# Sample attention in a decoder step: first values load issued ahead of the last unit's stores, last merge one entry later

## The reference

```python
def dilated_attn_sample(q, kv_all, past_rows, window, dil):
    ...
    s = jnp.einsum('bshe,bskhe->bshk', q, g[:, :, :, 0]).astype(jnp.float32) * ATTN_SCALE
    p, lse = masked_softmax_stats(s, valid[None, :, None, :])
    o = jnp.einsum('bshk,bskhe->bshe', p.astype(q.dtype), g[:, :, :, 1])
    return o, lse

def merge_dilation_groups(outs, lses):
    w = jax.nn.softmax(jnp.stack(lses, axis=0), axis=0)
    o = jnp.einsum('gblh,gblhe->blhe', w, jnp.stack(outs, axis=0).astype(jnp.float32))
```

## Time and profile before

| | |
|---|---|
| median of 3 runs | 2883.84 us |
| lowest, highest | 2879.44, 2885.67 us |
| span of the profiled execution | 2888.2 us |
| PE busy in it | 2766.8 us (96%) |
| DVE, ACT, POOL busy | 1331.5, 832.1, 822.3 us |
| DMA | 301.82 MB, mean 105 GB/s |

### The profile page before, as it was taken

How to read it: one execution, slowest core, us unless ns; L and a number is a source line. 1 busy time by engine, 2 the same in 40 slices (tenths; PEclk the granted TensorE clock), 3 DMA queues, 4 the chain that set the end, 5 groups by cost and what they waited for, 6 DMA issues and landing times.

```text
span 2888.2 us, 47476 instructions
## 1 busy us (share of the span) xinstructions
PE 2766.8 (96%) x18529; PEld 2633.0 (91%) x18529; DVE 1331.5 (46%) x2462; ACT 832.1 (29%) x1952; POOL 822.3 (28%) x505
## 2 busy tenths in 40 slices
PE   7999999999999999999999988989999999999997
PEld 5988998898899799999999977789999999999997
DVE  5477468647756851222323223277733333333334
ACT  5453154135325502323333322233400000000004
POOL 2342334324233423212212121123131313131322
PEclk9999999999999999999999998999999999999998
DMA  6533544333354431123232269972111111111111
GB/s 205 171 107 122 163 122 147 110 131 107 122 163 127 149 109 46 46 54 90 52 85 58 68 192 268 279 228 106 30 52 37 52 37 52 37 52 37 52 49 67
DMA packets 340262, 301.82 MB, mean 105 GB/s; under 512 B 25592, under 2 KB 308776, under 8 KB 338704
## 3 DMA queue, kind: packets, MB, share of 16 engines
q1 hardware_dynamic: 255744, 242.30, 27.6%
q10 hardware_dynamic: 84296, 56.40, 6.7%
HBM read 249.49 MB, written 102.91 MB: 122 GB/s over the span
## 4 chain that ended last, share of the span: by engine, by line
PE 85%; DVE 3%; DMA 3%; ACT 2%; issue 2%; SPq 2%; POOL 1%; ACTq 1%; DVEq 0%; POOLq 0%
PE ps L2145 23%; PE ps L2146 22%; PE ps L2147 22%; PE ps L2471 2%; PE ps L2447 2%; DMA kraw<-in_cache_kv_w_dram 1%; PE ps L2313 1%; PE ps L2309 1%; PE ps L2462 1%; PE ps L2153 1%; PE ps L2515 1%; PE ps L2154 1%; PE ps L2155 1%; PE ps L2312 1%; DMA wraw<-in_w_out_dram 1%
## 5 line engine op out<-in xcount | busy, mean ns | idle before, releaser
L2145 PE MATMUL ps<-hH,wH 128*128 128x384 f32 (+1 forms) x1896 | 636.1, 336 | 16.2 <-issue 5.2
L791 POOL CAST wH<-wraw 128x1024 fp32r<-128x1024 f32 (+2 forms) x186 | 195.1, 1049 | 1521.7 <-PE ps L2147 1164.1
L2146 PE MATMUL ps<-hL,wH 128*128 128x384 f32 (+1 forms) x1896 | 622.1, 328 | 0.0
L2147 PE MATMUL ps<-hH,wL 128*128 128x384 f32 (+1 forms) x1896 | 622.1, 328 | 0.0
L793 POOL TENSOR_TENSOR wL<-wraw,wH 128x1024 fp32r<-128x1024 f32 (+2 forms) x186 | 447.8, 2407 | 14.9
L2145 PEld LDWEIGHTS ps<-hH,wH 128*128 128x128 f32 x1896 | 359.3, 189 | 32.9 <-issue 23.3
L2145 PE MATMUL ps<-mH,wH 128*128 128x384 f32 (+1 forms) x1128 | 371.3, 329 | 3.6 <-issue 3.6
L2146 PE MATMUL ps<-mL,wH 128*128 128x384 f32 (+1 forms) x1128 | 370.8, 329 | 0.0
L2147 PE MATMUL ps<-mH,wL 128*128 128x384 f32 (+1 forms) x1128 | 370.2, 328 | 0.0
L2146 PEld LDWEIGHTS ps<-hL,wH 128*128 128x128 f32 x1896 | 359.5, 190 | 0.0
L2147 PEld LDWEIGHTS ps<-hH,wL 128*128 128x128 f32 x1896 | 358.8, 189 | 0.0
(11 more groups left out here) (386 smaller groups left out, 5038.6 us busy)
## 6 DMA issues: line engine op xcount, KB each, us to landing
wraw<-in_w_in_dram SPq DMA_DIRECT2D x92, 512.0 KB, 3.9
wraw<-in_w_up_dram SPq DMA_DIRECT2D x44, 512.0 KB, 3.7
ssdcr<-cum_scr ACTq DMA_DIRECT2D x32, 512.0 KB, 4.8
out_dram<-in_cache_kv_w_dram SPq DMA_DIRECT2D x16, 960.0 KB, 5.3
wraw<-in_w_down_dram SPq DMA_DIRECT2D x22, 512.0 KB, 3.2
kraw<-in_cache_kv_w_dram SPq DMA_DIRECT2D x40, 256.0 KB, 8.6
vraw<-in_cache_kv_w_dram SPq DMA_DIRECT2D x40, 256.0 KB
ssds<-in_state_ssm_dram ACTq DMA_DIRECT2D x16, 512.0 KB, 4.2
```

Source lines behind the costliest of these rows:

```text
L791: pool.tensor_copy(hi, a).then_inc(w_hi, 1)
L2145: pe.matmul(dst, hi, cols(mH[:, k, :], c), start=k == 0, stop=False)
L2146: pe.matmul(dst, hi, cols(mL[:, k, :], c), start=False, stop=False)
L2147: last = pe.matmul(dst, lo, cols(mH[:, k, :], c), start=False, stop=k == kt - 1)
```

## The change

Three things move; nothing is added to the work or taken from it, except one more wait on SP.

1. On SP, `load_v(0)` with its waits stands ahead of `send_unit(NJ - 1, 2)` and `merge_store(2)` instead of behind them. `load_new(0)` stays behind the stores, with an explicit wait for them.
2. `merge_load(NJ - 1)` moves from before entry 0's `load_new` to behind entry 2's K. The merge's steps on DVE and its exponential on ACT, which were in the second and third entry (`b` 1 and 2), come one entry later.
3. The load of `atok` from `a_scr` moves from behind entry 1's K to behind entry 4's K, that is, into the fourth pass of the loop. `load_gate_chunk(7)` stays where it was.

```diff
                     for y in range(3, 7):
                         load_gate_chunk(y)
-                    send_unit(NJ - 1, 2)
-                    merge_store(2)
                     sp.wait_ge(s_ready, tiles)
                     sp.wait_ge(vt_ready, tiles)
                     sp.wait_ge(kvn_out[1], 16 * 2)
                     load_v(0)
-                    merge_load(NJ - 1)
+                    send_unit(NJ - 1, 2)
+                    merge_store(2)
+                    sp.wait_ge(unit_out[2], 16 * 6 * NJ + 1)
                     load_new(0)
                     for b in range(DB - 1):
                         sp.wait_ge(k_fill, 12 * b + 9)
                         load_k(b + 1)
                         if b == 0:
+                            load_gate_chunk(7)
+                        if b == 1:
+                            merge_load(NJ - 1)
+                        if b == 3:
                             sp.wait_ge(pv_ready, tiles)
                             sp.wait_ge(a_out, 16 * (NJ - 1))
                             for j in range(NJ - 1):
                                 sp.dma_start(atok[:, :, j * P:(j + 1) * P], a_scr[j]).then_inc(at_in, 16)
-                            load_gate_chunk(7)
@@ ACT
-                if b == 1:
+                if b == 2:
                     merge_exp(NJ - 1)
@@ DVE, ahead of the wait for the exponential
-                if b == 1:
+                if b == 2:
                     merge_ops(NJ - 1, 1, 3)
-                if b == 2:
+                if b == 3:
                     merge_ops(NJ - 1, 9, 11)
```

## The result

The changed kernel takes 2865.58 us (median of 17 runs, 2859.16 to 2877.3) against 2885.67 us for the kernel before (median of 17 runs beside them). The ratio is 0.994, with a 95% interval of 0.9927 to 0.9952: 17 us faster, between 14 and 21. That is inside the range of the prediction and 4 us better than its number, -13.

A forecast was written before the change was run, and what follows sets the result against it. PE bounds nearly the whole span, but sample attention begins bound by transfers. Entry by entry -16.3 us, -12 with slower loads, taken as -13: 2870.8 us against the median 2883.84; range 2862 to 2879 for 8 in 10 runs.

The forecast's parts named there:

- The idle stretch and the first wait: Ahead of entry 0: DMA queue idle 12 us, then full; early values block starts the values product at 1722.6, not 1735.03: -12.4 us.
- The worst case for `vnew`: Entry 0: `vnew` takes 7.9 us as in a full queue, lands at 1726.5, gain 8.5 us instead of 12.4.
- The walk: Sample attention followed entry by entry with 8.4 us a load: -21.3 us at entry 2's keys, -16.3 at entry 4.
- a new wait in entry 3: Entry 3's keys land at 1772.3, behind the moved `mgb`; PE asks at 1767.7: a wait of 4.6 us.
- the wait for `pts`: PE's 1.98 us wait while DVE's merge products run beside POOL's split; moves from entry 2 to entry 3, size kept.
- POOL's quarter: DVE's three merge products, run alone, gain the same quarter as POOL's split (2.40 for 3.23): 4.8 us.
- The sum: Whole change: -16.3 us with loads of 8.4 us, -12 with slower transfers; -13 taken, so 2870.8 us.
- The queue has more room: Sample attention: entry 3's keys not late, products free of POOL, -21 to -23 us kept, 2863 to 2861; chance 0.12.
- Most is given back: DMA queue full from 1720 to entry 7's keys: gain only -4 to -9 us, 2875 to 2880; chance 0.18.
- The early block delays something: Last unit's stores late by 8.4 us: entry 0's gain shrinks to 4 us, no change, 2880; chance 0.04.
- DVE waits for the late `mgb`: Entry 2: late `mgb` holds DVE, then PE; gain used up if 16 us late; 2884 to 2892; chance 0.04.
- The rule beside the sum: Loads at about 358 GB/s per core: a block takes 6.6 us, no new wait arises, result about -20 us.

## Why the prediction was right, step by step

**The idle stretch and the first wait.** Right in what the sum used. (The worst case for `vnew`, given as 1726.5, is 1717.6 + 7.9 = 1725.5, and its gain 9.5 instead of 8.5; the sum doesn't use it.) The wait of 12.42 us is gone (the values product starts 16.2 us after the first keys; 1722.6 - 1706.28 = 16.3 were forecast). The trace has no landing time for the value block, but the queue was full up to the first store, at 1701.05, and not beyond: the DMA share is 1.03 from 1698 to 1700, 0.78 from 1700 to 1701 and 0.42 from 1701 to 1703. The stores were not late: DVE's wait for them ended 11.2 us after the first keys, 11.3 before. `vnew`, which was given up to 4 us in the worst case, cost nothing.

**The walk.** Time of each entry's first keys, counted from entry 0's (us; the last column is the product behind the stage):

| | entry 1 | entry 2 | entry 3 | entry 4 | entry 7 | next stage |
|---|---|---|---|---|---|---|
| before | 37.2 | 63.6 | 86.1 | 105.1 | 167.4 | 192.9 |
| forecast by the walk | 23.0 | 42.3 | 66.0 | 88.8 | 153.7 ("near 1860") | - |
| after, first profile | 22.4 | 43.8 | 68.0 | 91.6 | 150.6 | 175.5 |
| after, second | 24.1 | 43.2 | 66.5 | 89.0 | 153.9 | 181.0 |
| after, third | 23.0 | 43.6 | 67.1 | 89.4 | 155.9 | 181.4 |

The order of gains and debts is as forecast: a peak in entry 2, a new wait in entry 3 (4.6 forecast; 5.12, 4.08 and 4.45 measured), the wait for `pts` moved to entry 3 (1.98 forecast; 1.83 in all three). The run with the products in entry 4 shows the one debt to be POOL's split beside DVE, the run with `mgb` one entry on the other to be `mgb`'s place. One price in the walk was off: for the three products alone it had 4.8 us, from POOL's quarter, and they took 3.50.

**The sum.** The walk gave -16.3; I took 3 us off for a slower queue and said -13. This is the step that was mis-sized. The timed difference is -17 (14 to 21), so the walk's own number was the better one. The stretch from 1710 to 1770 ran at 290 GB/s (282 and 287 in the other two profiles), not at 271. The 271 of the earlier trace rows is a mean over a stretch that also holds the end of the unit's stores, and I had used it for loads of K and V: in the same trace of the kernel before, 1720 to 1780, past the stores and with `atok` still inside, has 282. The 240 GB/s taken for `mgb` and `atok` stands in no row of any run; with `mgb` inside, 1725 to 1765 of the changed kernel has 290. The profiles don't settle the rest. At entry 4 the three have -13.5, -16.1 and -15.8, at the next stage -17.5, -12.0 and -11.5: what differs is how long entries 6 and 7 wait for keys, 0.8 to 7.7 us in sum, in one and the same kernel. The assumption that both kernels wait the same there can be neither shown nor denied from one profile each.

**The rivals.** "The queue has more room" is off: the keys of entry 3 were late in every profile. "Most is given back" (-4 to -9) is off too, at -17. "The early block delays something" had no trace in any row. "DVE waits for the late `mgb`" did not happen: DVE began L1797 the moment its reduction was done. Something else that I did not foresee sits there, below. The rule beside the sum finds no support where it was applied: while the loads of keys and values fill the queue, the changed kernel's best row had 318 GB/s (1830 to 1860), and the new wait that the rule would have denied arose. In other traffic the rate was higher: 351 GB/s from 1850 to 1880 in the run with `atok` last, where gates, weights and `accm` are loaded too. The rule is that of the Trainium skill, HBM Reference, section Specifications (TRN2), with about 358 GB/s per core.

**Which part brought it.** By the timed runs the value block is worth 7.5 us alone, `mgb` and `atok` together 10.7, `atok` in that 4 to 8. The rival of the given-back gain called the block of 2.36 MB the only real gain in bytes; that is right for a queue that is full to the end, but `mgb` and `atok` also left the full stretch for the middle one, where the share rose from 0.84 to 0.95.

## What to carry to other kernels

Where the profile shows an engine waiting for a transfer, look past the named one to what stands ahead of it in the queue, and look for an idle stretch of the same queue right before: a block moved there alone was worth about its own length here (7.5 us for 8.4), and a walk entry by entry with one measured load time forecast the next four entries within 3 us. Inside the full stretch, moving `mgb` one entry on only moved the wait, and spreading it gave nothing that could be measured. Whether taking bytes out of the stretch helps by itself is not shown: the two runs that did so can't be told from the change by their times, and only the third, which also put the next stage's weights first, is likely ahead of it. It pays to look at who is next in line, since a stage that ends earlier also asks earlier for what stands behind it. Where two profiles of one kernel differ by as much as the step that is judged, only the timed runs decide.

## What the runs showed of the hardware

Some steps of DVE seem to be held by POOL for as long as its instruction lasts. In the changed kernel, steps 1 and 2 of the merge ran beside a POOL split and took 1.00 and 2.34 us; in the kernel before, the first stood at 0.18. The rows of DVE and then of POOL, changed kernel:

```profile
1754.49 1.00 DVE L1797 TENSOR_TENSOR mgmin<-mgb 128x16 f32<-128x16 f32 x1
1755.64 2.34 DVE L1800 TENSOR_TENSOR mgmin<-mgmin,mgb 128x16 f32<-128x16 f32 x1
```

```profile
1754.42 1.04 POOL L794 CAST wH<-wraw 128x1024 fp32r<-128x1024 f32 x1 [0.20 <-POOL qblk L910]
1755.55 2.40 POOL L796 TENSOR_TENSOR wL<-wraw,wH 128x1024 fp32r<-128x1024 f32 x1
```

The second step ends with POOL's row (1757.98 and 1757.95), and POOL's keeps its usual 2.40. The first step ends with POOL's first (1755.49 and 1755.46), too. The same pair of times shows in all ten other profiles in which these steps meet a split (0.97 to 1.01 and 2.33 to 2.34); in the three in which they don't, both take 0.17 or 0.18. It is not their small size: in the fourteen profiles the reciprocal of 128x1 (L1901) stood beside a split twelve times and took 0.16 or 0.17 us, against 0.15 to 0.17 in most other places, and the copies of 128x512 from `ps` (L1883) took 0.69 us beside a split and apart from it. The steps that were held are those with two input tensors of which neither lies in `ps`; that of 128x512 with one of the two in `ps` (L1906) took 0.69 us beside a split, as apart from it. Beside the three large products it was the other way too: POOL's split went from 2.40 to 3.24 us. That the two engines share something, and that two such inputs are what counts, is a reading of these rows; no run took it apart.

PE's clock fell after short waits as well as long ones, and not after every one. Entry 1's keys in the changed kernel came after a wait of 1.88 us and took 4.07 us, at a mean granted clock of 0.65; in its second profile they came after 3.23 us and took 2.53:

```profile
1723.40:1728.30 4.90, 4.83 (x26) 4.84 (x27) 1.38 (x2) 1.76 (x3) 0.00 (x0) 0.65 1.08 370
```

```profile
1729.26 2.53 PE L2518 MATMUL ps<-ident,kraw 128*128 128x128 f32 x20 [3.23 <-DMA kraw<-in_cache_kv_w_dram]
```

So a row of a product behind a wait is no sure price for that product: both 2.5 us and 4.5 us (entry 7's keys behind the wait of 5.66) are to be had.
